# Features dealt to partitions in runs of eight in the expert stage of a diffusion block, on one Trainium2 core

## What is computed

```python
h = modulate(rms_norm(x, norm2_w), sh2, sc2)          # h * (1 + scale) + shift, per feature
# for each expert e, with the rows of h that were routed to it (xb: rows x 1024):
y = (silu(xb @ exp_w1[e]) * (xb @ exp_w3[e])) @ exp_w2[e]   # w1, w3: 1024 x 512; w2: 512 x 1024
out[token] += gate * y
```

## Time and profile before

| | |
|---|---|
| median of 3 executions | 3097.43 us |
| the profiled execution | 3096.11 us |
| its span, first to last instruction | 3094.0 us |
| TensorE busy in the span | 2624.5 us (85%) |
| VectorE, ScalarE, GpSimd busy | 1299.9, 1085.1, 680.2 us |
| moved by DMA | 472 MB, mean 153 GB/s |
| mean granted TensorE clock | 0.908 of full |

### The profile page before, as it was taken

How to read it: one execution, slowest core, us unless ns; L and a number is a source line. 1 busy time by engine, 2 the same in 40 slices (tenths; PEclk the granted TensorE clock), 3 DMA queues, 4 the chain that set the end, 5 groups by cost and what they waited for, 6 DMA issues and landing times. The chain is left out here.

```text
span 3094.0 us, 40387 instructions
## 1 busy us (share of the span) xinstructions
PE 2624.5 (85%) x12691; PEld 1750.5 (57%) x12692; DVE 1299.9 (42%) x2250; ACT 1085.1 (35%) x2054; POOL 680.2 (22%) x1351
## 2 busy tenths in 40 slices
PE   5879999999677959768999999970988898886997
PEld 1326444444445445447998899860655565554664
DVE  5634671221122314132344554420746565453664
ACT  2542111111221211212344545410645565443563
POOL 2640110000000000006145555553122212222221
PEclk8989999999888979875799999965999999998999
DMA  5972211110499696761011111103886798765793
GB/s 183 330 212 72 52 45 31 52 55 28 129 245 222 149 233 156 175 186 34 29 58 54 54 54 58 58 35 124 312 286 208 246 330 286 233 205 181 239 351 113
DMA packets 307937, 472.00 MB, mean 153 GB/s; under 512 B 26852, under 2 KB 195180, under 8 KB 300996
## 3 DMA queue, kind: packets, MB, share of 16 engines
q1 hardware_dynamic: 229815, 396.89, 40.3%
q0 software_dynamic: 18416, 44.58, 6.3%
q10 hardware_dynamic: 59616, 29.38, 3.5%
HBM read 370.64 MB, written 108.05 MB: 155 GB/s over the span
## 5 line engine op out<-in xcount | busy, mean ns | idle before, releaser
L798 PE MATMUL ps_proj<-sb_hT,sb_win 128*128 128x512 f32 x768 | 336.1, 597 | 7.6 <-DVE sb_rot L903 6.0
L798 PEld LDWEIGHTS ps_proj<-sb_hT,sb_win 128*128 128x128 f32 x768 | 145.7, 192 | 189.9 <-issue 183.0
L2191 PE MATMUL ps_byp<-sb_w,sb_gT 128*128 128x512 f32 x512 | 236.0, 604 | 3.9 <-ACT sb_gT L2006 3.9
L1917 DVE TENSOR_TENSOR sb_w1l<-sb_raw,sb_w1h 128x1024 fp32r<-128x1024 f32 x128 | 148.2, 1220 | 167.8 <-ACT sb_w1h L1978 167.8
L1407 POOL MEMSET sb_pr<- 128x1026 int32 x1 | 1.0, 958 | 907.7 <-POOLq L186 907.7
L1686 DVE CUSTOM_DVE_ANT_0 sb_pr<-ps_S,sb_mask 128x640 f32<-128x640 f32 x128 | 105.6, 825 | 216.8 <-PE ps_S L1535 216.6
L1204 DVE TENSOR_TENSOR sb_ab<-sb_ab,ps_prod 128x512 f32<-128x512 f32 x64 | 44.1, 689 | 356.1 <-ACT sb_ab L1180 356.1
L1555 PE MATMUL ps_O<-sb_v,sb_pt 128*128 128x64 f32 (+1 forms) x1280 | 176.0, 293 | 0.0
L1555 PEld LDWEIGHTS ps_O<-sb_v,sb_pt 128*128 128x128 f32 x1280 | 173.3, 214 | 0.0
L1614 ACT COPY sb_pt<-ps_PT 128x512 f32<-128x512 f32 x128 | 74.6, 583 | 275.5 <-PE ps_PT L1541 275.4
L1917 DVE TENSOR_TENSOR sb_w3l<-sb_raw,sb_w3h 128x1024 fp32r<-128x1024 f32 x128 | 150.5, 1217 | 0.7 <-ACT sb_w3h L1978 0.5
(11 more groups left out here) (291 smaller groups left out, 5658.3 us busy)
## 6 DMA issues: line engine op xcount, KB each, us to landing
sb_raw<-in_exp_w SPq DMA_DIRECT2D x64, 2048.0 KB, 17.5
sb_w<-in_exp_w SPq DMA_DIRECT2D x32, 2048.0 KB, 9.1
sb_ada<-in_ada_w SPq DMA_DIRECT2D x16, 1536.0 KB, 8.1
scr_filt<-sb_fout ACTq DMA_DIRECT2D x128, 128.0 KB, 4.5
sb_yh<-scr_filt SPq DMA_DIRECT2D x32, 512.0 KB, 11.2
scr_hy_y<-sb_sp SPq DMA_DIRECT2D x32, 512.0 KB
sb_yx<-scr_hy_y SPq DMA_DIRECT2D x32, 512.0 KB, 7.9
scr_hy_v<-sb_yx SPq DMA_DIRECT2D x64, 256.0 KB, 4.3
```

Of the source, the lines that this page charges most:

```text
L798: ins = pe.matmul(mp[:, (NQ + n) % 4, :], w[:, pc % 3, k, (ct % 2) * P:(ct % 2 + 1) * P], g.hT[:, k, c * 512:(c + 1) * 512], start=(k == 0 ...
L1917: ve.tensor_tensor(piece(low[m], part), piece(raw13[par][:, m], part), piece(high[m], part).bitcast(F32), ALU.subtract).then_inc(lo[m], 1)
L2191: ins = pe.matmul(yp[:, part, :], gT[:, f, :], w2[par][:, f, part * 512:(part + 1) * 512], start=(f == 0), stop=(f == FT - 1), skip_group_ ...
```

## The change

A feature 8 p + k now belongs to partition p, run k, in the rows and in w1 and w3. A partition's part of w1 or of w3 is then one piece of 16 KB. The transposes read every eighth column of the gathered rows. The columns of scale and shift must be dealt in the same way, so ScalarE writes the two tables (1024 values each) to a scratch tensor in HBM at the start of the stage, value by value, waits, and reads them back as `mod2`, 64 bytes a partition in two runs; ScalarE and VectorE wait for that before the first tile is scaled. w2, the hidden features and the output keep their places.

```diff
+        mod2 = e.sb(st, "mod2", [P, 2, KT])
...
+        mod_dram = e.dram("mod2", [2, D])
...
         def load13(eng, ex, par, m):
-            src = i[("exp_w1", "exp_w3")[m]][0, bass.ds(ex, 1)].rearrange("a (k p) f -> p (a k) f", p=P)
+            src = i[("exp_w1", "exp_w3")[m]][0, bass.ds(ex, 1)].rearrange("a (p k) f -> p (a k) f", p=P)
             eng.dma_start(raw13[par][:, m, :, :], src).then_inc(ldw13[m][par], 16)
...
                 for k in range(4):
-                    ins = ve.tensor_scalar(xf[:, k, :], tpp[:, 0, k, :], g.scale2[:, k:k + 1],
-                                           g.mods[:, 0, 24 + k:25 + k], ALU.mult, ALU.add)
+                    ins = ve.tensor_scalar(xf[:, k, :], tpp[:, 0, k, :], mod2[:, 0, k:k + 1],
+                                           mod2[:, 1, k:k + 1], ALU.mult, ALU.add)
...
+            ve.wait_ge(mod_in, 16)
             scaled(0)
...
         def _(act):
+            for c, m in enumerate((g.scale2[:, :], g.mods[:, 0, 24:24 + KT])):
+                act.dma_start(mod_dram[c].rearrange("(k p) -> p k", p=P), m, allow_slow_non_contiguous=True).then_inc(mod_out, 16)
+            act.wait_ge(mod_out, 32)
+            act.dma_start(mod2[:, :, :], mod_dram.rearrange("c (p k) -> p c k", p=P)).then_inc(mod_in, 16)
...
-                                         bias=g.mods[:, 0, 24 + k:25 + k], scale=g.scale2[:, k:k + 1])
+                                         bias=mod2[:, 1, k:k + 1], scale=mod2[:, 0, k:k + 1])
...
+            act.wait_ge(mod_in, 16)
             scaled(0)
...
                 for k in ks:
-                    ins = pe.transpose(tpp[:, k // 4, k % 4, :], xg[:, k * P:(k + 1) * P], g.ident[:, :])
+                    ins = pe.transpose(tpp[:, k // 4, k % 4, :], xg[:, k::KT], g.ident[:, :])
                 return ins
```

More of the change, by code:

```diff
@@ L1819, in stage6 @@
         added = e.sem("s6_tiles_added")
+        mod_out = e.sem("s6_modulation_stored")
+        mod_in = e.sem("s6_modulation_loaded")
         tt = e.sem("s6_rows_turned")
```

## The result

The changed kernel takes 3133.3 us (median of 4 executions, 3125.3 to 3136.6). The kernel before takes 3099.3 us (median of 4, 3096.2 to 3107.2). The ratio is 1.0102, with a 95% interval of 1.0075 to 1.0129, so the change costs 34 us by the medians and 23 to 40 us by the interval. The profiled execution has a span of 3134.5 us.

A forecast was written before the change was run, and what follows sets the result against it. It took the chain of additions and gathers around lots, slowed by loads beside them, to bound the expert stage. Terms -2 - 2 + 21 + 3 + 1.7 = +21.7, taken as +21, gave 3118 us against the median; range 3084 to 3150.

The forecast's parts named there:

- Gathers and additions beside the loads: Expert stage: small transfers alternate packets with 16 KB pieces, 3.2 us more each with enough load left; +21 us, bounds -15 to +55.
- The tables' way through HBM: Start of the expert stage: scale and shift tables return at 2158, hidden by 4 us; cost 0, bounds 0 and +12 us.
- Clock: TensorE in the expert stage: one or two longer waits newly reach the lower clock; +3 us, bounds 0 to +8.
- Transposes: Row transposes reading every eighth float: 424 x 4 ns = 1.7 us; upper bound 23 us from exposed weight loads.
- Loads: w1 and w3: 0.7 us less a pair, -2 us on the chain, -2 us for records and first weights; bounds 0 to -8.
- Whole loads in front: Rival: gathers wait for a whole load, +7.7 us at six places, about +50 us, 3147; chance 0.16 together with late start.
- Faster: Rival: engines share by bytes, gathers' wait before the first row halves at eight places; -12 us, 3085; chance 0.22.
- Start: Rival: tables come late and delay the first tile by 10 us, on top of any other; chance 0.16 together with whole loads.

The follow-up runs named there:

- b_16k: Kernel before with only the w1 and w3 loads made in runs of 16 KB a partition: 3119.1 us, +19.1 us over before.
- b_16k_again: Kernel before with only the 16 KB runs of w1 and w3, measured once more: 3126.8 us, +25.8 us over before.
- a_early: Changed kernel with the scaling tables sent to HBM in the stage before and read back at its end: 3124.5 us, +27.3 us over the kernel before.
- b_stride: Kernel before with only the row transposes reading every eighth column: 3096.6 us, -0.6 us against before.
- a_order_early: Changed kernel with tables sent in the stage before and the gather issued ahead of the wait for the addition: 3069.0 us, -28.2 us against the kernel before.
- b_order: Kernel before with the next gather issued before GpSimd waits for the previous tile's addition to land: 3065.3 us, -31.9 us against before.
- b_tables: Kernel before with only the scaling tables sent through HBM and back: 3110.0 us, +10.0 us over before.
- a_2k_early: Changed kernel with loads in 2 KB pieces by unused floats and tables sent in the stage before: 3100.0 us, -3.4 us against the kernel before.

## Why the prediction was right, and where it was not

The direction was right (slower), and 3133.3 us lies in the range of 3084 to 3150. The forecast of 3118 us was too low: +21 us against +34. By its steps:

- **Gathers and additions beside the loads, +21 us.** Right in mechanism, and the total is met within the scatter; its parts are not all. Contended gathers came at 11.6, 10.9 and 11.1 us, 3.1, 3.8 and 2.9 us longer than before for the 3.2 that I took, and with the same wait before the first row (4.6 and 4.8 us), as I had left it. The wait for gathered rows is 58.4 us where I had said about 58. Additions came at up to 13.63 us, above the 9 to 12 that I named: a single one is delayed by 4.9 us instead of 3.2 (8.74 to 13.63). The gather behind it is then freed of the load, and the pair costs 2.3 us where I took 1.3 (2.6 for two such places). The last gather, for which I took half the price, came in sooner than before (5.22 to 4.35 us). That the sum still fits is in part luck. The pieces alone gave +19.1 and +25.8 us in two runs, with everything they bring, clock and quicker loads too; by the prediction's terms that is 21 + 3 - 4 = 20 us.
- **The tables' way through HBM, 0 us.** This is the step that failed. I let the stores land like g2row, after 13.6 us, and called the way hidden by 4 us. They took 18.2 and 21.7 us, the load back 9.4, and the first scaled tile came at 2170.75, not near 2161; 2165 was the point that I had named as wrong. Of the 2170.75, 3.5 us are the later start of the stage, and without them it is still 2167.2. The upper bound in the step, +12 us, gave the reason: 2048 values of 4 bytes are much slower than their bytes. The step also looked only at who waits for the tables. What it missed is whom their packets hold up: the records' load took 12.7 us from 2145.66 to 2158.4 instead of 6.7 (8.8 in b_16k, so some 2 us of it go with the long pieces), and the first gather was issued 3.5 us later in the stage. Its transposes end at 2169.6, so the tables themselves, there at 2170.73, add about 1 us to what the late gather costs. Alone the way costs 10.0 us; in the changed kernel the profile shows 5.0, and its removal is worth 6.7 us by the medians, within the intervals of the two runs. Issues of the changed kernel on ScalarE's queue:

```profile
2139.59 0.60 ACTq L1981 DMA_DIRECT2D scr_mod<-sb_mods  x1
2161.30 0.37 ACTq L1983 DMA_DIRECT2D sb_mod<-scr_mod  x1
2170.75 1.50 ACT L1992 ACTIVATE sb_bxf<-ps_btp,sb_mod 128x128 f32<-128x128 f32 x4 [49.21 <-DMA sb_mod<-scr_mod]
```

- **Clock, +3 us.** Too small. From the first product to the end TensorE is busy for 810.15 us where it was 796.35, for the same instructions, at a mean granted clock of 0.92 instead of 0.94 (the changed kernel's stretch, then that of before):

```profile
2174.80:3134.50 959.70, 810.15 (x4552) 539.45 (x4552) 509.18 (x748) 473.08 (x748) 190.79 (x228) 0.92 0.69 240
```

```profile
2166.30:3094.00 927.70, 796.35 (x4552) 524.97 (x4552) 509.70 (x748) 472.44 (x748) 188.95 (x228) 0.94 0.75 249
```

  Of these 13.8 us some 7 are the transposes themselves (309 ns in the mean instead of 292, x 424), which run right behind the waits. In b_16k it is 5.7 us (802.1), in b_16k_again 7.8 (804.1), so with the strides a part of the 13.8 may not be clock. Already the first main tile ran at a clock of 0.92 and took 21.3 us; it had 1.00 and 19.7 us before. The late start is not the reason, since a_early starts as before and has the same 0.92 and 21.3 us there, and b_16k has 1.00 and 19.6; what made it stays open:

```profile
2189.50:2210.80 21.30, 20.70 (x77) 14.44 (x77) 11.33 (x17) 11.58 (x18) 4.40 (x5) 0.92 0.62 243
```

- **Transposes, +1.7 us.** By themselves nothing that can be measured (-6 to +4 us), beside long pieces perhaps 4 us. The weight load came to 191 ns, near the 196 of the row that I went by. Here the rule of the Trainium skill ("SBUF — State Buffer", section "Door 1: The DMA port swizzle") and the measurement part: the penalty that it names is seen in the weight load, 50 ns, and the estimate of 23 us by that rule is excluded by b_stride.
- **Loads, -2 and -2 us.** A pair of loads gained more than I took: it lands 1.6 us sooner in the median of the 16 that can be compared, and 2.6 to 3.1 us sooner at the three places that were in the chain (17.34 to 14.24 us for the longest), where I had reckoned 0.7 us from the packets' own durations. It is worth little: on the chain a load now stands once (14.24 us) instead of three times, because later gathers and additions stand in its place. In a_order_early, with the gathers mostly out of the way, no gain over b_order is left either (3069.0 and 3065.3 us).
- **Rivals.** *Whole loads in front* (3147) falls: the contended gathers are 2.9 to 3.8 us longer and not 7.7, and the queues' packets are one for one, 79 to 75. The rule of the Trainium skill behind it ("DMA: Bandwidth & Descriptors", section "Queues, rings and completion order"), a change of queue only after some 9 to 17 descriptors, is not what this trace shows; had it held, all 16 packets that a pair of loads has on an engine could have gone ahead of the gather's. *Faster* (3085) falls with it: the gathers beside a fresh load (the three above) came in at 10.9 us and more, not below 7, and their wait before the first row did not shrink. *Start* was half right and deserved a term in the sum instead of a chance beside it; with its 5 to 10 us the forecast would have been 3123 to 3128.

The measured parts add up within their spread: 19 to 26 us for the pieces with their clock, 5 to 10 us for the tables, 0 to 4 for the strides, 24 to 40 in all, against 34 (23 to 40) for the whole.

## What to carry to other kernels

Where small transfers in the critical chain share the DMA engines with bulk loads, the length of the bulk's pieces is their price: here each of their packets waited for about one long packet, and loads that land 1.6 us sooner made the kernel slower. Before trading piece lengths, ask why the small transfer is in the chain at all; here moving one wait behind the next gather's issue was worth 32 us, more than the whole effect of the pieces in either direction. A table rearranged element by element through HBM belongs in a stage where nothing waits: here its price was less when it arrived than whom its 2048 packets delayed.

## What was unexpected of the hardware

- 4 KB stored as 1024 pieces of 4 bytes beside the loads landed after 16.5 us, the next one after 26.8 us (b_tables), and a load of the records beside them took 12.6 instead of 6.7 us.
- The same tables cost the start 5.0 us beside pieces of 16 KB, 10.7 beside 2 KB, 17.9 beside 2 KB into a padded tile, where SyncE stood 13.6 us at one issue, and 11.5 beside 8 KB into a padded tile, where it stood 0.6 us there but the records' load took 20.0. SyncE's issue behind the first two loads took 3.7 to 4.5 us with 2 KB pieces and 0.4 us with 16 KB, so short pieces were kind to gathers and held up the issuing queue. Padding alone does not make the 13.6 us: in a_2k_early, without the tables, it was 4.1. One profile each; why padding and tables together cost so much is open.
- In an undisturbed stretch the DMA engines were busy for 0.82 instead of 0.89 of the time with the loads in longer pieces (287 and 297 GB/s), and yet additions between main tiles took longer: the one issued at 2529.24 landed after 13.3 us, its pair of before (2506.68) after 8.6.
